# First layer's modulation vectors: a third of the columns in the opening stage, two thirds at two seams of the attention stage

## What is computed

```python
act_c = jax.nn.silu(c);  act_cc = jax.nn.silu(c_ctx)
for i in range(DEPTH):                                   # DEPTH = 2
    mod_l = (act_c @ w_mod[i] + b_mod[i]).reshape(bsz, 6, 1, d)
    sh1, sc1, ga1, sh2, sc2, ga2 = [mod_l[:, j] for j in range(6)]
    mod_c = (act_cc @ w_mod[i] + b_mod[i]).reshape(6, d)
    csh1, csc1, cga1, csh2, csc2, cga2 = [mod_c[j] for j in range(6)]
    p_l = ada_norm(x, g_mix[i], sh1, sc1) @ w_in[i]      # needs columns 0 to 2047 of the modulation
    ...                                                  # attention A and B, recurrence C
    x = x + ga1 * (concatenate([ya_l, yb_l, yc_l]) @ w_out[i])   # needs columns 2048 to 3071
    f_l = ada_norm(x, g_ffn[i], sh2, sc2)                # needs columns 3072 to 5119
    ...                                                  # mixture of experts
    x = x + ga2 * y                                      # needs columns 5120 to 6143
```

## Time and profile before

| what | us |
|---|---|
| median of 3 runs (4845.9 to 4850.27) | 4847.15 |
| the profiled execution's own time | 4848.02 |
| its span in the trace | 4846.0 |
| modulation stage, from the start to the first instruction of the next stage | 78.77 |
| attention stage of layer 0, first key load issued to the first instruction of the scan stage | 660.47 to 1038.14 |

### The profile page before, as it was taken

One profiled execution on the slowest core, in us unless ns is written; L12 is line 12 of the kernel. 1 busy time (PEld: TensorE's weight loads), 2 busy tenths in 40 slices (PEclk: granted clock), 3 DMA queues, 4 the chain that ended last, 5 costly groups with the idle time before them and its releaser, 6 DMA issues. The chain is left out here.

```text
span 4846.0 us, 90034 instructions
## 1 busy us (share of the span) xinstructions
PE 4058.8 (84%) x38594; PEld 2401.3 (50%) x38594; DVE 2163.2 (45%) x2888; ACT 1195.2 (25%) x1971; POOL 509.7 (11%) x522
## 2 busy tenths in 40 slices
PE   4998979979999796999938988799689988688893
PEld 1443545658888453443414444366578874333341
DVE  1465437755666543111133654377566656310014
ACT  0221127742322110101001211177332322100001
POOL 0232310001000100000021323200000000000001
PEclk7999968989999897999968999799899999799996
DMA  8467441024332755998976665500323214499996
GB/s 339 129 174 202 134 120 29 23 65 128 103 106 78 277 232 234 402 405 355 396 293 206 171 205 156 131 24 23 98 58 90 65 49 175 198 385 388 390 428 237
DMA packets 252294, 932.77 MB, mean 192 GB/s; under 512 B 37076, under 2 KB 100500, under 8 KB 223264
## 3 DMA queue, kind: packets, MB, share of 16 engines
q1 hardware_dynamic: 205752, 756.31, 42.2%
q0 software_dynamic: 28704, 117.20, 8.4%
q10 hardware_dynamic: 17480, 53.95, 2.8%
HBM read 722.31 MB, written 165.77 MB: 183 GB/s over the span
## 5 line engine op out<-in xcount | busy, mean ns | idle before, releaser
L806 PE MATMUL ps<-w,hT 128*128 128x480 f32 (+3 forms) x2240 | 885.9, 555 | 1.4 <-ACT hT L611 1.4
L2644 PE MATMUL ps<-w,xT 128*32 128x512 f32 (+2 forms) x3104 | 669.1, 612 | 68.3 <-DMA w<-in_e_w 59.7
L806 PEld LDWEIGHTS ps<-w,hT 128*128 128x128 f32 x2240 | 435.5, 198 | 430.7 <-issue 407.8
L2587 DVE TENSOR_TENSOR sg<-sg,ps 128x512 f32<-128x512 f32 x46 | 31.6, 687 | 975.3 <-ACT sg L2375 975.3
L2644 PEld LDWEIGHTS ps<-w,xT 128*32 128x32 f32 (+2 forms) x3104 | 239.1, 137 | 459.7 <-issue 447.0
L1118 DVE TENSOR_REDUCE nm<-ps 128x1 f32<-128x1280 f32 (+1 forms) x216 | 295.8, 1370 | 145.7 <-PE ps L1209 145.7
L1209 PE MATMUL ps<-KT,qs 32*128 32x512 f32 (+3 forms) x1200 | 288.8, 600 | 50.5 <-DMA ident<-in_k_ident 24.4
L2644 PE MATMUL ps<-w,hT 128*32 128x512 f32 (+2 forms) x1552 | 324.9, 594 | 3.5 <-ACT hT L2366 3.5
L1076 ACT ACTIVATE work<-ps,nm 128x1280 f32<-128x1280 f32 (+1 forms) x216 | 265.9, 1231 | 97.2 <-DVE nm L1118 93.1
L2120 PE MATMUL ps<-w_out,yT 128*128 128x512 f32 x576 | 256.7, 604 | 14.6 <-ACT yT L1960 14.6
L594 ACT ACTIVATE po<-ps 128x480 f32<-128x480 f32 (+3 forms) x140 | 75.2, 539 | 657.2 <-PE ps L806 648.9
(11 more groups left out here) (326 smaller groups left out, 5318.4 us busy)
## 6 DMA issues: line engine op xcount, KB each, us to landing
w<-in_e_w SPq DMA_DIRECT2D x192, 2048.0 KB, 20.2
wt<-in_w_mod SPq DMA_DIRECT2D x8, 3072.0 KB, 25.1
w_mod<-in_w_mod POOLq DMA_DIRECT2D x3, 8192.0 KB, 31.2
s_ye<-yo ACTq DMA_DIRECT2D x46, 512.0 KB, 10.8
w<-in_w_in SPq DMA_DIRECT2D x12, 1920.0 KB, 14.3
ra<-s_scan SPq DMA_DIRECT2D x160, 128.0 KB, 2.8
kb<-s_scan SPq DMA_DIRECT2D x160, 128.0 KB, 2.9
x<-s_x SPq DMA_DIRECT2D x36, 512.0 KB, 6.9
```

The source lines that it names most:

```text
L806: mm = pe.matmul(ps[:, c, a - c0:b - c0], hT[i % 2][:, t, :], w[:, c, t, a - c0:b - c0], start=(t == 0), stop=(t == DT - 1))
L2644: mm = pe.matmul(ps[lo:hi, bank, :], xs[:, t, lo:hi], w[p % 3][:, t, cols], start=(t == 0), stop=(t == nt - 1), skip_group_check=len(tiles ...
```

## The change

The modulation stage now makes columns 0 to 2047 alone: 8 slices of 1024 KB, each in its own buffer and with its own semaphore, 4 products a slice into the four strips of one bank, one add on 128 x 512, four stores. The bank and the bias tile are cleared first, since the add now reads all partitions.

In the attention stage of layer 0, POOL loads columns 2048 to 4095 with one DMA of 8192 KB right behind V, clears the bias tile and loads eight bias pieces. PE multiplies them (32 products into bank 4) between the last `back` of `ctx` and the first `fill` of `lat`; DVE adds the bias behind the last `normalise` of `ctx`; the second `fill` of `lat`, which writes banks 3 to 5, waits for that add. POOL then loads columns 4096 to 6143 into the same buffer, PE multiplies them into bank 1 behind the last `back` of `lat`, DVE adds, and POOL stores all eight pieces at the stage's end. The attention stage of layer 1 has the same instructions as before.

```diff
@@ modulation_phase @@
+        wt = sb("wt", [P, DT, MOD_GROUP])
+        bias, res = sb("bias", [P, MOD_W]), sb("res", [P, MOD_W])
...
-                for n in range(DT):
-                    if n >= WB:
-                        sp.wait_ge(w_used, n - WB + 1)
-                    src = ins["w_mod"][0].rearrange("(p t) n -> p t n", t=DT)[:, n, :]
-                    sp.dma_start(wt[n % WB][:], src).then_inc(w_in[n % WB], 16)
+                for t in range(DT):
+                    sp.dma_start(wt[:, t, :], mod_weights(net, 0, 0)[:, t, :]).then_inc(w_in[t], 16)
...
-                for c in range(NCH):
-                    q = slice(32 * (c % QC), 32 * (c % QC) + 2)
-                    dve.tensor_tensor(chunk(res, c), ps[q, c // QC, :], chunk(bias, c), ALU.add).then_inc(added, 1)
+                dve.wait_ge(mod_ps, 1)
+                dve.tensor_tensor(res[:], ps[:, 0, :], bias[:], ALU.add).then_inc(added, 1)
...
+                for t in range(DT):
+                    pe.wait_ge(w_in[t], 16)
+                    for c in range(MOD_Q):
+                        mm = pe.matmul(ps[mod_strip(c), 0, :], act[:, t, :], wt[:, t, c * MOD_W:(c + 1) * MOD_W],
+                                       start=(t == 0), stop=(t == DT - 1))
+                mm.then_inc(mod_ps, 1)
@@ attention_phase @@
+        LATE = [1, 2] if layer == 0 else []
+        MOD_BANK = [4, 1]
...
                 pool.dma_start(V[:], net.v.rearrange("(t p) n -> p t n", p=P)).then_inc(v_in, 16)
...
+                def load_group(k):
+                    if k > 0:
+                        pool.wait_ge(mod_ps, k)
+                    pool.dma_start(w_mod[:], mod_weights(net, layer, LATE[k])).then_inc(w_mod_in, 16)
+
+                if LATE:
+                    load_group(0)
+                    pool.memset(bias[:], 0.0).then_inc(bias_clear, 1)
+                    pool.wait_ge(bias_clear, 1)
+                    for k, g in enumerate(LATE):
+                        for c in range(MOD_Q):
+                            src = ins["b_mod"][layer][mod_columns(g, c)].partition_broadcast(2)
+                            pool.dma_start(bias[mod_strip(c), k, :], src).then_inc(bias_in, 16)
...
                     tiles(pool, pt.n, tile)
+                    if LATE and n == 0:
+                        load_group(1)
+                for k, g in enumerate(LATE):
+                    pool.wait_ge(mod_added, k + 1)
+                    for c in range(MOD_Q):
+                        pool.dma_start(net.mod[layer][:, mod_columns(g, c)], res[mod_strip(c), k, :]
+                                       ).then_inc(mod_stored, 16)
+                if LATE:
+                    pool.wait_ge(mod_stored, 16 * MOD_Q * len(LATE))
...
+                def add_bias(k):
+                    if k == 0:
+                        dve.wait_ge(bias_in, 16 * MOD_Q * len(LATE))
+                    dve.wait_ge(mod_ps, k + 1)
+                    dve.tensor_tensor(res[:, k, :], ps[:, MOD_BANK[k], :], bias[:, k, :], ALU.add).then_inc(mod_added, 1)
...
                     tiles(dve, pt.n, tile)
+                    if LATE:
+                        add_bias(n_part)
...
+                def modulate(k):
+                    pe.wait_ge(w_mod_in, 16 * (k + 1))
+                    for t in range(DT):
+                        for c in range(MOD_Q):
+                            mm = pe.matmul(ps[mod_strip(c), MOD_BANK[k], :], net.act[:, t, :],
+                                           w_mod[:, t, c * MOD_W:(c + 1) * MOD_W], start=(t == 0), stop=(t == DT - 1))
+                    mm.then_inc(mod_ps, 1)
...
                             fill(i, par, 0, nth)
+                            if LATE and pt.k0 > 0:
+                                pe.wait_ge(mod_added, 1)
                             fill(i, par, 1, nth)
...
                     tiles(pe, pt.n, tile)
+                    if LATE:
+                        modulate(n_part)
```

More of the change, by code:

```diff
@@ L189, in __init__, with mod_strip, mod_weights, mod_columns @@
         self.ye = nc.dram_tensor("s_ye", [NB * P, D], F32).ap()
-def modulation_phase(nc, net, ps):
[L196 to L200, removed]
+MOD_W, MOD_Q = 512, 4
+MOD_GROUP = MOD_W * MOD_Q
+def mod_strip(c):
+    return slice(32 * c, 32 * c + 2)
+def mod_weights(net, layer, g):
+    cols = slice(g * MOD_GROUP, (g + 1) * MOD_GROUP)
+    return net.ins["w_mod"][layer].rearrange("(p t) n -> p t n", t=DT)[:, :, cols]
+def mod_columns(g, c):
+    return slice((g * MOD_Q + c) * MOD_W, (g * MOD_Q + c + 1) * MOD_W)
+def modulation_phase(nc, net, ps):
     ins = net.ins
@@ L205, in modulation_phase @@
         act = net.act
-        wt = [sb(f"wt{b}", [P, 6 * D]) for b in range(WB)]
-        bias = sb("bias", [P, NBK, NW])
-        res = sb("res", [P, NBK, NW])
+        wt = sb("wt", [P, DT, MOD_GROUP])
+        bias, res = sb("bias", [P, MOD_W]), sb("res", [P, MOD_W])
         cond_in, sig_done, act_done, b_in = sem("cond_in"), sem("sig_done"), sem("act_done"), sem("b_in")
-        w_in = [sem(f"w_in{b}") for b in range(WB)]
-        w_used, added, stored = (sem(n) for n in ("w_used", "added", "stored"))
-        chunk = lambda t, c: t[32 * (c % QC):32 * (c % QC) + 2, c // QC, :]
+        w_in = [sem(f"w_in{t}") for t in range(DT)]
+        bias_clear, bank_clear, mod_ps, added, stored = (
+            sem(n) for n in ("bias_clear", "bank_clear", "mod_ps", "added", "stored"))
         def store(eng, first):
-            for c in range(first, NCH, 2):
-                eng.wait_ge(added, c + 1)
-                eng.dma_start(net.mod[0][:, c * NW:(c + 1) * NW], chunk(res, c)).then_inc(stored, 16)
+            eng.wait_ge(added, 1)
+            for c in range(first, MOD_Q, 2):
+                eng.dma_start(net.mod[0][:, mod_columns(0, c)], res[mod_strip(c), :]).then_inc(stored, 16)
         with nc.Block() as block:
@@ L234, in _ @@
                 act_e.activation(sig[:], cond[:], ACT.Sigmoid).then_inc(sig_done, 1)
[L235 to L237 removed]
+                act_e.wait_ge(bias_clear, 1)
+                for c in range(MOD_Q):
+                    src = ins["b_mod"][0][mod_columns(0, c)].partition_broadcast(2)
+                    act_e.dma_start(bias[mod_strip(c), :], src).then_inc(b_in, 16)
@@ L246, in _ @@
-                dve.wait_ge(w_used, DT)
-                for c in range(NCH):
-                    q = slice(32 * (c % QC), 32 * (c % QC) + 2)
-                    dve.tensor_tensor(chunk(res, c), ps[q, c // QC, :], chunk(bias, c), ALU.add).then_inc(added, 1)
+                dve.wait_ge(b_in, MOD_Q * 16)
+                dve.wait_ge(mod_ps, 1)
+                dve.tensor_tensor(res[:], ps[:, 0, :], bias[:], ALU.add).then_inc(added, 1)
             @block.tensor
             def _(pe):
+                pe.wait_ge(bank_clear, 1)
@@ L927, in attention_phase @@
         minus_half = sb("minus_half", [P, 4])
+        LATE = [1, 2] if layer == 0 else []
+        MOD_BANK = [4, 1]
+        if LATE:
+            w_mod = sb("w_mod", [P, DT, MOD_GROUP])
+            bias, res = sb("bias", [P, len(LATE), MOD_W]), sb("res", [P, len(LATE), MOD_W])
+        bias_clear, bias_in, w_mod_in, mod_ps, mod_added, mod_stored = (
+            sem(s) for s in ("bias_clear", "bias_in", "w_mod_in", "mod_ps", "mod_added", "mod_stored"))
         ident_in, k_more = sem("ident_in"), [sem(f"k_more{g}") for g in range(GROUPS)]
```

13 lines of the change are left out of this document (8 added, 5 removed).

## The result

The changed kernel takes 4825.9 us (median of 8 runs, 4816.4 to 4838.1), where the kernel before takes 4846.6 (8 runs, 4840.0 to 4857.3). The ratio is 0.9958 with a 95% interval of 0.9942 to 0.9974: 20.7 us less, 12.6 to 28.1 by the interval. The forecast was 44 less, and 4825.9 lies above its range (4797 to 4820). The profiled execution was one of the fastest, 4816.4 with a span of 4814.1.

A forecast was written before the change was run, and what follows sets the result against it. The opening stage was taken as bound by the transfer of 24576 KB of weights, the `ctx` part by PE at the lower clock with full DMA engines. Terms -49.5 + 1 - 0.5 + 5 = -44 gave 4803 us, range 4797 to 4820.

The forecast's parts named there:

- The opening stage: Modulation stage: slices of a third the size, each 2.48 us, next stage beginning at 29.3; gain 49.5 us.
- The first load and the `ctx` part: Layer 0 attention, context part: load lands by 722, before PE needs it; cost between 0 and 12.9 us, taken as 1.
- The seam: Between `ctx` and `lat`: products take 8.9 us, first maximum 6.2 later, lifted clock saves 6.8; net taken as -0.5 us.
- the rival in which the clock falls again: At the seam: clock rises in the products, falls in PE's pause; +6.2, total 4810; one of two forms sharing chance 0.12.
- The end: End of layer 0 attention: second group's products, add, POOL's four stores and barrier lengthen the stage by 5 us.
- the first load collides: Rival, context part or seam: second context tile's queries or the load land late; total 4805 to 4816; chance 0.11.
- does not shrink to a third: Rival, opening stage: rows of 8 KB move slower than rows of 24 KB; gain 41.7, total 4811; chance 0.03.
- slower than before: Rival, seam: PE stands waiting for the first load, landing later than 768; chance 0.02.
- gives nothing back: Rival, seam: the clock falls again (+6.2, total 4810) or never rises (+12.5, total 4816); chance 0.12.

## Why the prediction was wrong

- **The opening stage**: 49.5 forecast, 50.1 measured, by its own steps (slices of 2.50, one add of 0.69, two stores a queue). The term was right.
- **The step that failed: "The first load and the `ctx` part"**, taken at +1, between 0 and 12.9; it measured +17.0 and +16.7 in two profiles. The reasoning had two faults. It counted demand (all has landed by 722, however the queues share) and took the queries' 6.9 us to spare as enough, because V stands ahead of the load. That V is safe is true; but for the queries what counts is the share of SP's queue once V is through, and this is small when the other queue holds rows of 8 KB: 22 KB a us, so 6 us for each load of 128 KB. The second fault is the bound: 12.9 was the load's 19.8 us at 429 GB/s less the slack, but the load took 33.7 us to land, and the last of the queries landed no earlier.
- **What could have been read beforehand**: the prediction weighed the rule of the Trainium skill on turns by packets against the change and set it aside, because V beside the keys in rows 5 "does not settle it". The landings in rows 5 do not, but the packets in the same trace do. From 680 to 682, V in q0 and keys and queries in q1:

```profile
q0 software_dynamic: 146, 0.67, 93.0%
q1 hardware_dynamic: 142, 0.07, 12.4%
```

Packet for packet, 4.6 KB against 0.5. With packets of 8.2 KB on the other side, SP's queue gets 0.5 of every 8.7 KB; of 429 GB/s that is 25 KB a us, 5.3 us for a query load. An estimate from these rows: the first lands 8.8 us behind its issue as before and four more follow, 675.33 + 8.8 + 4 x 5.3 = 705, which is 11 us behind the 694.30 at which they are needed. That is near the upper end, not +1. It measured 17, in part because the engines moved 381 to 389 GB/s and not 429; the rest is open.
- **The seam**: -0.5 forecast; +8.6 - 8.4 = +0.2 measured, +0.1 in the second profile. The products began low and rose, 8.62 and 7.89 us for 8.9. The first maximum came 6.0 us later relative to the stage's start, the wait on the queries left out (6.2 forecast), and from it to POOL's step 5.8 came back (6.8 forecast). The step held in both parts, but that both profiles met it so closely is partly luck: the clock did fall for a while behind the pause (0.66 and 0.69 in a stretch). In three other kernels with the same products the seam and first tile together, waits left out, cost some 6 (load behind the queries), 5 (load in SP's queue) and 6 us (short rows), which is about the +6.2 of the rival in which the clock falls again.
- **The end**: +5 forecast, +7.0 measured. Mis-sized: from the last add to the next stage the forecast had 2.0 + 1.6 + 0.8 = 4.4 us for POOL's four stores; it is 6.45.
- **Sum**: with 17.0, 0.2 and 7.0 in place of 1, -0.5 and 5 the forecast would have been -25, total 4822, against 4825.9 measured with an interval of some 8 us to each side. The rival "the first load collides" was the right one; it had a chance of 0.11 and a total of at most 4816, because its price had the same wrong bound.
- The time fell, as forecast. Nothing in the rivals "does not shrink to a third" or "slower than before" came true; "gives nothing back" did not in the two profiles of the changed kernel, but did in part in its variants. With the collision taken away and the stores moved, the same idea gives -45.1, the size that was forecast, though partly through another tail.

## What to carry to other kernels

When a large load is moved beside small transfers that someone needs soon, total demand says only when the last byte lands; ask which queue each stands in and how long the rows are, and put the load in the queue of the urgent ones, behind them. A trace of the kernel before shows the share: compare the packets and bytes of each queue in a stretch in which both are at work. Count the slack of every transfer in flight, not only of the one that you add. A stage that ends in a barrier pays its last stores in full: issue them from the queue with the shortest end.

## What the runs showed of the hardware

- One load of 8192 KB with rows of 8 KB in one queue held five query loads of 128 KB in another from 8.8 us to as much as 32 (the second context tile started 35.3 us after the first query load was issued); with rows of 2 KB the wait fell from 17 to 5.7 us, with both in one queue and the queries ahead it was nil.
- Queues at work together moved the same number of packets: 438 and 439 in 10 us with the load in POOL's queue, 302, 301 and 301 with three queues, 627 and 628 in 8 us with short rows. Packets held one row of 8 KB, two rows of 2 KB, three rows of V (4.6 KB), or one row of 0.5 KB.
- The load issued by ACT's queue delays V and queries alike (10.5 and 3.9 us): the queue's kind made no difference to the sum (14.4, against 14.2 to 16.8 from POOL's).
- The end of a stage behind four stores of 4 KB issued by POOL is 6.45 us from the last add (6.9 in the profile with short rows), behind two each from SP and ACT 2.9.
- 64 records of products with two stationary columns lifted PE's clock from 0.50 within their 7.6 to 10.0 us in every profile, and the clock fell again, to 0.50 for 10 us in one, after PE's pause of 1.98 us for the first maxima of the next tile.
